# First attention: VectorE takes the row maxima two items ahead before it combines the two maps of the next item

## The chip, the cores and the metric

One core of a Trainium2 chip runs the kernel. The metric is the time of one execution on the device in microseconds; lower is better. "PE" is TensorE, "DVE" VectorE, "ACT" ScalarE, "POOL" GpSimd.

## The reference

Two transformer blocks, one after the other, on 1024 tokens of width 1024. The change is in the first one's differential attention: four heads, 1040 keys (16 meta tokens ahead of the 1024), two maps of scores with 64 dimensions each, values of 128.

```python
def diff_attention(q1, q2, k1, k2, v, lam):
    def block(args):
        q1b, q2b, start = args
        causal = k_pos[None, :] <= q_pos[:, None]
        def probs(qb, k):
            s = jnp.einsum('bhqd,bhkd->bhqk', qb, k, preferred_element_type=jnp.float32) * scale
            return jax.nn.softmax(jnp.where(causal, s, -jnp.inf), axis=-1)
        attn = probs(q1b, k1) - lam * probs(q2b, k2)
        return jnp.einsum('bhqk,bhkd->bhqd', attn, v32)
```

Around it stand normalisations, a state space branch, an output projection and a gated feed-forward part; the second block has a gating unit, a second attention with one map, and a feed-forward part of its own. None of these is changed.

## The kernel before

Each engine has its own program, and semaphores order them. The first attention is the object att1 of the class Attention (line 2108, `maps == 2`). Its work is cut into 32 items: 4 heads times 8 tiles of 128 queries. Item (h, i) has 16 + 128 (i + 1) key columns: 144 for the first tile of a head, then 272, 400, 528, 656, 784, 912 and 1040. The keys of an item are cut into tiles of 128 and one of 16, and these go in batches of up to four: items with up to three whole tiles have one batch, the next four sizes two, the longest three.

For one item n the work is, in order:

- scores: TensorE, `pe_scores` (lines 1546 and 1551, the mask), both maps, into PSUM banks 0 to 2 and 3 to 5. Each map has one place for scores, so the scores of n wait for both exponentials of n-1;
- maxima: VectorE, `dve_max` (line 1648), one TENSOR_REDUCE for each map; it waits for the scores;
- exponentials with their row sums: ScalarE, `act_exp` (line 1623), one for each map; they wait for the maxima;
- combination: VectorE, `dve_prob` (lines 1666, 1667, 1669): a reciprocal, a small product (rho), and one long instruction that adds the second map times rho to the first; it waits for both exponentials;
- turns: TensorE, `pe_turn` (line 1562), transposes a batch; the first batch of an item waits for the combination;
- copy: ScalarE, `evacuate` (lines 1609 and 1613), from PSUM to SBUF;
- product with V: TensorE, `pe_pv` (line 1576), after the copy;
- scale: VectorE, `dve_out` (line 1683), after the item's last product.

The order on each engine is written out by hand, as a loop over n. In step n TensorE does the scores of n+2, and then for each batch b of item n the turn of batch b+1 and the product of batch b; so the turn of the first batch of item n+1 comes ahead of the last product of item n. ScalarE copies the same batches, up to the first one of n+1, and then does the exponentials of n+2. VectorE does the combination of n+1, the maxima of n+2 and the scale of n. Of the 32 steps the last two have no item n+2, and the very last has no item n+1. The second attention uses the same class with one map and has no combination.

Of the kernel before, what the change touches and what calls it, by code (L numbers as in the profile page):

```python
# [66 lines left out]
def _program(nc, io, ctx):  # L67
# [286 lines left out]
    class Turn:  # L354
# [43 lines left out]
        def dve(self, v, link):  # L398
            g = self.nseg
            seg = self.width // self.nseg  # L400
            per = self.nk // 4
            n = 0
            for i in range(self.tiles + 1):
                if i < self.tiles:
                    w = self.w(i)
                    if i == 0:
                        v.wait_ge(self.sq, (self.turn + 1) * self.tiles * g)
                        rsqrt(v, link, *(t[:, 0:self.tiles, 0:g] for t in (stat, rst, tmpa, tmpb)),
                              self.nseg / self.width, EPS, self.factor)
                    if i >= 2:  # L410
                        v.wait_ge(self.turned, self.n0() + per * (i - 1))
                    for s in range(self.nseg):
                        c = slice(s * seg, (s + 1) * seg)
                        ins = v.scalar_tensor_tensor(self.xs[0:w, i % 2, c], self.src(i)[:, c],
                                                     rst[0:w, i, s:s + 1], self.gain[0:w, c], ALU.mult, ALU.mult)
                    ins.then_inc(self.scaled, 1)
                if i >= 1:
                    w = self.w(i - 1)
                    for b in range(0, self.nk, 4):
                        v.wait_ge(self.hi, self.n0() + n + 1)  # L420
                        cols = slice(self.cols(i - 1), self.cols(i - 1) + w)
                        v.tensor_tensor(self.dst(b, 1)[:, :, cols],
                                        ps[:, self.bank(n), 0:4 * w].rearrange("p (k c) -> p k c", k=4),
                                        self.dst(b, 0)[:, :, cols].bitcast(F32), ALU.subtract).then_inc(self.lo, 1)
                        n += 1
# [1033 lines left out]
    class Attention:  # L1459
# [225 lines left out]
        def dve(self, v, link):  # L1685
            N = len(self.items)
            self.dve_max(v, 0, link)
            self.dve_max(v, 1, link)
            if self.maps == 2:
                self.dve_prob(v, 0, link)  # L1690
            else:
                self.evacuate(v, nc.vector.tensor_copy, 0)
            for n in range(N):
                if self.maps == 2 and n + 1 < N:
                    self.dve_prob(v, n + 1, link)
                if n + 2 < N:
                    self.dve_max(v, n + 2, link)
                for b in self.steps(n):
                    if self.maps == 1 and b % 2 == 0:
                        self.evacuate(v, nc.vector.tensor_copy, b)  # L1700
                self.dve_out(v, n, link)
# [1213 lines left out]
```

## Time and profile before

| | |
|---|---|
| median of 3 runs | 2657.24 us (2650.01 to 2657.88) |
| the profiled execution | 2656.39 us |
| its span | 2654.6 us |
| PE busy in the span | 2442.3 us (92%) |
| DVE busy in the span | 1487.2 us (56%) |
| ACT busy in the span | 796.5 us (30%) |
| maxima of the first attention, first and last start | 304.4 and 469.9 us |
| scale of the first attention, last start | 483.1 us |

The profile is of one execution. The span runs from its first instruction to its last, and all times of rows are counted from its start. An engine's busy time leaves out its waits; TensorE's is modelled, since matmuls overlap. The granted clock of TensorE is 1.00 at 2.4 GHz and 0.50 at 1.2 GHz.

### The profile page before, as it was taken

The page shows a single profiled execution, that of the slowest core. Times are in us where ns is not written, and L with a number is a line of the kernel's source. Part 1 is how long each engine was busy: PE and PEld are TensorE (multiplying, and loading weights), DVE is VectorE, ACT ScalarE, POOL GpSimd, SP SyncE. Part 2 cuts the span into 40 slices and gives each one's busy share as a digit, 9 for nine tenths or more (in the row PEclk, how much of TensorE's full clock was granted, in tenths as well). Part 3 has the DMA queues.
Part 4 walks back from the last instruction along what each step waited for, and adds up shares of the span by engine and source line. Part 5 has one row for each costly group of instructions (what it writes and reads, how often), then busy time and mean ns, then how long its engine had stood idle before and what let it go on. Part 6 is the DMA issues. An engine that isn't in the chain of part 4 may idle for free.

```text
span 2654.6 us, 33063 instructions
## 1 busy us (share of the span) xinstructions
PE 2442.3 (92%) x11846; PEld 1983.5 (75%) x11846; DVE 1487.2 (56%) x2086; ACT 796.5 (30%) x1512; POOL 1130.1 (43%) x867
## 2 busy tenths in 40 slices
PE   8998877389799999999989999889989999999996
PEld 7976755277588888888868887677868888888885
DVE  5984656443565555655564610665555555555556
ACT  4321344513422222222233101443442222222222
POOL 3220130025365555665575424100635555655553
PEclk8998899689999999999999999999989999999998
DMA  5446410011221111111142212100321111111114
GB/s 141 123 134 163 154 40 1 4 56 56 88 60 48 47 47 59 55 51 47 48 152 92 64 32 74 62 1 1 127 68 48 48 54 54 58 47 47 50 58 143
DMA packets 177348, 179.50 MB, mean 68 GB/s; under 512 B 39752, under 2 KB 139976, under 8 KB 177248
## 3 DMA queue, kind: packets, MB, share of 16 engines
q1 hardware_dynamic: 171376, 163.96, 20.4%
q10 hardware_dynamic: 5872, 14.22, 1.6%
q8 instruction: 61, 1.00, 0.2%
q14 instruction: 39, 0.32, 0.0%
HBM read 147.65 MB, written 30.49 MB: 67 GB/s over the span
## 4 chain that ended last, share of the span: by engine, by line
PE 81%; DVE 7%; ACT 5%; issue 3%; POOL 2%; DMA 2%; SPq 0%; ACTq 0%; POOLq 0%; DVEq 0%
PE ps L267 23%; PE ps L269 22%; PE ps L268 22%; PE ps L1546 3%; PE ps L1576 3%; PE ps L1562 2%; ACT ex L1623 2%; PE ps L562 1%; DVE hbuf L513 1%; PE ps L1551 1%; DVE hbuf L2051 1%; PE ps L1437 1%; PE ps L2613 1%; PE ps L2565 1%; PE ps L1452 1%
## 5 line engine op out<-in xcount | busy, mean ns | idle before, releaser
L2051 DVE TENSOR_TENSOR hbuf<-hbuf,ps 128x1024 f32<-128x1024 f32 x320 | 390.7, 1221 | 254.0 <-PE ps L269 233.7
L207 POOL TENSOR_TENSOR wgt<-raw,ones 128x512 fp32r<-128x512 f32 x76 | 86.7, 1141 | 573.1 <-PE ps L269 418.3
L267 PE MATMUL ps<-mlp_dh,mlp_fh 128*128 128x512 f32 x672 | 264.4, 393 | 12.8 <-POOL mlp_dzl L1852 10.0
L269 PE MATMUL ps<-mlp_dh,mlp_fl 128*128 128x512 f32 x672 | 263.3, 392 | 0.0
L268 PE MATMUL ps<-mlp_dl,mlp_fh 128*128 128x512 f32 x672 | 262.7, 391 | 0.0
L1839 POOL TENSOR_TENSOR mlp_s_raw<-mlp_gh_raw,mlp_s_raw 128x512 f32<-128x512 f32 x44 | 57.2, 1299 | 284.1 <-PE ps L269 284.1
L267 PEld LDWEIGHTS ps<-mlp_dh,mlp_fh 128*128 128x128 f32 x672 | 126.6, 188 | 43.7 <-POOL mlp_dzl L1852 10.8
L268 PEld LDWEIGHTS ps<-mlp_dl,mlp_fh 128*128 128x128 f32 x672 | 126.7, 189 | 27.5
L269 PEld LDWEIGHTS ps<-mlp_dh,mlp_fl 128*128 128x128 f32 x672 | 126.5, 188 | 27.7
L1852 POOL TENSOR_TENSOR mlp_dl<-mlp_d_raw,mlp_dh 128x1024 fp32r<-128x1024 f32 x42 | 113.7, 2706 | 46.7 <-ACT mlp_dh L2028 46.7
L1546 PE MATMUL ps<-k,q 64*128 64x512 f32 (+6 forms) x416 | 89.8, 534 | 45.1 <-ACT ex L1623 43.8
L2088 DVE TENSOR_TENSOR mlp_fl<-mlp_p,mlp_fh 128x512 fp32r<-128x512 f32 x42 | 114.4, 2723 | 3.7
L209 POOL TENSOR_TENSOR wgt<-raw,wgt 128x512 fp32r<-128x512 f32 x76 | 104.2, 1371 | 6.0
L1839 POOL TENSOR_TENSOR mlp_s_raw<-mlp_gl_raw,mlp_ul 128x512 f32<-128x512 f32 x44 | 57.2, 1300 | 116.0 <-PE ps L269 116.0
L1562 PE MATMUL ps<-ident,ex 128*128 128x128 f32 (+1 forms) x464 | 82.8, 291 | 17.3 <-ACT ex L1623 14.8
L1655 DVE CUSTOM_DVE_ANT_0 ex<-ps,negc 128x128 f32<-128x128 f32 (+7 forms) x64 | 48.3, 754 | 81.2 <-PE ps L1551 80.6
L267 PE MATMUL ps<-x1h,chunk_w 128*128 128x352 f32 (+2 forms) x256 | 89.6, 350 | 2.5 <-DVE x1l L713 1.6
L1546 PEld LDWEIGHTS ps<-k,q 64*128 64x128 f32 x416 | 38.3, 199 | 69.3 <-issue 39.1
L1985 ACT CAST mlp_s3h<-mlp_s_raw 128x512 fp32r<-128x512 f32 x44 | 27.5, 625 | 202.6 <-POOL mlp_s_raw L1839 202.6
L269 PE MATMUL ps<-x1h,chunk_w 128*128 128x352 f32 (+2 forms) x256 | 87.9, 343 | 0.0
L268 PE MATMUL ps<-x1l,chunk_w 128*128 128x352 f32 (+2 forms) x256 | 87.8, 343 | 0.0
L1609 ACT COPY at<-ps 128x512 f32<-128x512 f32 (+3 forms) x96 | 43.2, 450 | 133.0 <-PE ps L1562 133.0
(485 smaller groups left out, 6812.5 us busy)
## 6 DMA issues: line engine op xcount, KB each, us to landing
h<-hbuf SPq DMA_DIRECT2D x24, 512.0 KB, 2.9
mlp_d_raw<-in_w_down SPq DMA_DIRECT2D x21, 512.0 KB, 3.5
mlp_d_raw<-in_w_ffn_out SPq DMA_DIRECT2D x21, 512.0 KB, 3.3
raw<-in_w_in SPq DMA_DIRECT2D x40, 256.0 KB, 3.0
raw<-in_w_out SPq DMA_DIRECT2D x32, 256.0 KB, 2.8
res_b<-h SPq DMA_DIRECT2D x16, 512.0 KB, 4.3
mlp_ul<-in_w_up SPq DMA_DIRECT2D x22, 256.0 KB, 3.1
mlp_uh_raw<-in_w_up SPq DMA_DIRECT2D x22, 256.0 KB, 3.4
```

The costliest lines, as they stand in the source:

```text
L207: nc.gpsimd.tensor_tensor(wh[:, s, :], r, ones[:, 0:1].broadcast_to([P, 512]), ALU.mult).then_inc(w_hi, 1)
L209: nc.gpsimd.tensor_tensor(wl[:, s, :], r, wh[:, s, :].bitcast(F32), ALU.subtract).then_inc(w_split, 1)
L267: pe.matmul(out, lhs[0], rhs[0], start=first, stop=False, skip_group_check=over)
L268: pe.matmul(out, lhs[0], rhs[1], start=False, stop=False, skip_group_check=over)
L269: return pe.matmul(out, lhs[1], rhs[0], start=False, stop=last, skip_group_check=over)
L1546: pe.matmul(self.score(item, m, a, b), self.q[rows, t, i * P:(i + 1) * P], self.k[rows, t, a:b], start=True, stop=True)
L1562: t = pe.transpose(ps[0:w, self.tbank(b), j * P:(j + 1) * P], self.ex[:, n % 3, 0, c:c + w], ident[:, :])
L1576: mm = pe.matmul(self.obank(n), self.atb[0:w, b % 3, j, :], self.v[0:w, t, h * self.dv:(h + 1) * self.dv], start=first, stop=last, skip_gr ...
L1839: nc.gpsimd.tensor_tensor(blk[name][2][:, :, :], x[:, :, :], y[:, :, :], op).then_inc(self.s["sums"], 1)
L1852: nc.gpsimd.tensor_tensor(self.d[z][1][:, :], self.d_raw[z][:, :], self.d[z][0][:, :].bitcast(F32), ALU.subtract).then_inc(self.s["split"], 1)
L2051: v.tensor_tensor(self.acc[:, i, :], self.acc[:, i, :], src, ALU.add).then_inc(self.s["added"], 1)
L2088: v.tensor_tensor(self.f[b][1][:, c], src, self.f[b][0][:, c].bitcast(F32), ALU.subtract)\
```

## The change

In step n VectorE's two calls change places: first the maxima of item n+2, then the combination of item n+1. Nothing else is changed; the second attention has no combination, and its order stays as it is.

```diff
@@ -1691,10 +1691,10 @@
             else:
                 self.evacuate(v, nc.vector.tensor_copy, 0)
             for n in range(N):
+                if n + 2 < N:
+                    self.dve_max(v, n + 2, link)
                 if self.maps == 2 and n + 1 < N:
                     self.dve_prob(v, n + 1, link)
-                if n + 2 < N:
-                    self.dve_max(v, n + 2, link)
                 for b in self.steps(n):
```

## Rows read from the trace of the kernel before

**Rows 1.** Stretches: PE, PEld, DVE, ACT, POOL busy (instructions), granted clock, DMA share, GB/s.
```profile
304.00:325.00 21.00, 15.43 (x63) 8.60 (x60) 8.93 (x23) 7.24 (x23) 0.99 (x1) 0.51 0.63 161
325.00:390.00 65.00, 45.29 (x323) 32.56 (x322) 40.64 (x72) 30.47 (x78) 29.34 (x24) 1.00 0.16 50
386.60:390.00 3.40, 1.51 (x15) 1.38 (x16) 1.62 (x4) 2.04 (x5) 0.00 (x0) 0.99 0.00 0
390.00:393.40 3.40, 3.40 (x17) 3.18 (x16) 0.69 (x3) 1.65 (x7) 0.00 (x0) 0.50 0.02 5
```

**Rows 2.** Waits from 304 to 484 us: total, times, longest.
```profile
PE ps L1546 <- ACT ex L1623: 43.8, 29, 2.7
...
DVE rl L1666 <- ACT ex L1623: 30.7, 27, 1.7
DVE negmax L1648 <- PE ps L1551: 26.9, 25, 6.0
...
PE ps L1562 <- DVE ex L1669: 2.5, 3, 1.6
ACT ex L1623 <- DVE negmax L1648: 2.2, 1, 2.2
```

**Rows 3.** The chain of waits from 404 to 475 us, shares by line.
```profile
by line: PE ps L1546 26.7%; ACT ex L1623 25.2%; issue 14.3%; PE ps L1562 12.6%; PE ps L1576 12.5%; PE ps L1551 4.4%; DVE ex L1669 1.9%; ACT at L1609 1.4%; ACT at L1613 0.8%; DVE rho L1667 0.4%; DVE rl L1666 0.3%; ACTq L1606 0.1%; DVEq L1665
```

**Rows 4.** Timeline of one round: start, duration, engine, line, operation.
```profile
418.79 0.17 DVE L1666 RECIPROCAL rl<-psum_l 128x2 f32<-128x2 f32 x1 [1.73 <-ACT ex L1623]
...
418.83 1.80 PE L1546 MATMUL ps<-k,q 64*128 64x512 f32 x8 [2.16 <-ACT ex L1623]
...
419.30 1.03 DVE L1669 SCALAR_TENSOR_TENSOR ex<-ex,rho 128x784 f32<-128x784 f32 x1
...
420.83 2.12 DVE L1648 TENSOR_REDUCE negmax<-ps 128x1 f32<-128x912 f32 x2 [0.50 <-PE ps L1551]
...
421.81 0.60 PE L1562 MATMUL ps<-ident,ex 128*128 128x128 f32 x4
...
422.93 1.03 ACT L1623 ACTIVATE ex<-ps,negmax 128x912 f32<-128x912 f32 x1
...
425.19 0.70 PE L1546 MATMUL ps<-k,q 64*128 64x512 f32 x2 [2.15 <-ACT ex L1623]
```

**Rows 5.** Timeline, the same instructions at other sizes.
```profile
433.03 1.30 DVE L1669 SCALAR_TENSOR_TENSOR ex<-ex,rho 128x1040 f32<-128x1040 f32 x1
...
434.25 0.52 DVE L1648 TENSOR_REDUCE negmax<-ps 128x1 f32<-128x144 f32 x2
...
434.47 0.60 PE L1562 MATMUL ps<-ident,ex 128*128 128x128 f32 x4
...
437.50 0.79 DVE L1648 TENSOR_REDUCE negmax<-ps 128x1 f32<-128x272 f32 x2
...
439.70 0.38 PE L1562 MATMUL ps<-ident,ex 128*128 128x128 f32 x2
...
450.93 0.61 PE L1562 MATMUL ps<-ident,ex 128*128 128x128 f32 x4
451.07 1.59 DVE L1648 TENSOR_REDUCE negmax<-ps 128x1 f32<-128x656 f32 x2 [0.34 <-PE ps L1551]
...
468.74 2.39 DVE L1648 TENSOR_REDUCE negmax<-ps 128x1 f32<-128x1040 f32 x2 [1.04 <-PE ps L1551]
...
469.84 0.60 PE L1562 MATMUL ps<-ident,ex 128*128 128x128 f32 x4
```

**Rows 6.** Timeline, scores of 656 columns and the next ones, at either clock.
```profile
407.00 2.56 PE L1546 MATMUL ps<-k,q 64*128 64x512 f32 x8 [0.60 <-ACT ex L1623]
...
413.01 1.59 PE L1546 MATMUL ps<-k,q 64*128 64x512 f32 x8 [1.27 <-ACT ex L1623]
...
449.50 1.37 PE L1546 MATMUL ps<-k,q 64*128 64x512 f32 x8 [1.31 <-ACT ex L1623]
...
453.90 0.70 PE L1546 MATMUL ps<-k,q 64*128 64x512 f32 x2 [1.27 <-ACT ex L1623]
```

## Prediction

> **What bounds the kernel now.** Only the first attention, about 304 to 484 us of the span, is touched, so I read that stretch: first the busy times and the granted clock by stretch, then the waits, the chain, and the timeline of single items. TensorE is busy for 45.29 of the 65 us from 325 to 390 [rows 1], so it is not full, and VectorE (40.64) is still less so. Nobody is short of throughput here; the stage is a ring of short waits. In the list of waits [rows 2] TensorE's scores wait for ScalarE's exponentials (43.8 us), VectorE for both (30.7 and 26.9 us). The two rows that matter most are the small ones. TensorE's turns wait for VectorE's combination 3 times, 2.5 us in all, and the exponential waits for the maxima once, 2.2 us. So today both VectorE results are nearly always ready before somebody asks. The chain of waits says the same: from 404 to 475 us scores, exponentials, turns and the product with V make it up, and VectorE's combination has 1.9% of it [rows 3].
>
> One round of the ring is in [rows 4], the step in which the scores have 912 columns and the combination 784. The exponentials of item n+1 end, and at 418.8 both TensorE (scores of n+2, to 420.8) and VectorE (reciprocal, rho, combination, 418.79 to 420.33) start. They run beside each other. VectorE then waits 0.50 us for the scores and takes both maxima, 420.83 to 422.95. Meanwhile TensorE does what is left of item n and begins at 421.81 to turn the first batch of n+1, which needs the combination; that has been ready since 420.33. ScalarE copies this batch out and at 422.93 starts the exponentials of n+2; the next scores follow at 425.19. The round takes 6.36 us. The maxima lie beside the turn and the copy, the combination beside the scores: the two VectorE parts have separate cover.
>
> **The change, part by part.** No instruction is added or removed; in each of the 30 steps that have an item n+2 the two maxima move ahead of the three combination instructions. No DMA moves, and VectorE's queue holds nothing else. What is new is a wait: VectorE takes its queue in order (in [rows 4] the maxima stand behind the combination), so the combination of n+1 now stands behind the wait for the scores of n+2 and behind both maxima. Behind the combination stand the turn of the first batch of n+1 on TensorE (with it the last product of n), its copy on ScalarE, and, queued behind that copy, the exponentials of n+2, and for these the scores of n+3 wait. The ring becomes one string: scores, maxima, combination, turn, copy, exponentials.
>
> The cost D of a step is the time by which the turn comes later. Counted from the start of the maxima it would start after M (both maxima) + 0.6 (reciprocal and rho, 418.79 to 419.30, and 0.1 of hand-overs) + P (combination), and it starts now after W:
> - 912 columns: 2.12 + 0.6 + 1.03 - (421.81 - 420.83 = 0.98) = 2.8 us [rows 4].
> - 656 columns: item n has a single batch, so the turn starts 0.14 before the maxima: 1.59 + 0.6 + 0.77 + 0.14 = 3.1 us; P is read off a line through 1.03 at 784 columns and 1.30 at 1040, 0.135 for each 128 [rows 4, 5].
> - 1040 columns: 2.39 + 0.6 + 1.17 (same line) - (469.84 - 468.74 = 1.10) = 3.1 us [rows 5].
> - 784, 528, 400 columns, M along the line from 0.52 at 144 to 2.39 at 1040: 1.86 + 0.6 + 0.90 - 0.9 = 2.5; 1.32 + 0.6 + 0.64 + 0.1 = 2.7; 1.06 + 0.6 + 0.50 + 0.1 = 2.2. (The 0.9 is W of the 912 step, a little less.)
> - 144 columns, behind the longest combination: the scores end by about 433.3 and the turn starts at 434.47 [rows 5]; 0.52 + 0.6 + 1.30 (the 1040 combination) - 1.2 = 1.2 us.
> - 272 columns, beside the longest item: TensorE has 2.2 us of work of item n (437.50 to 439.70 [rows 5]) and VectorE needs 0.79 + 0.6 + 0.36 = 1.8. This one is covered; if TensorE's work were not there it would cost 1.8.
>
> The six long sizes give 16.4 us a head, four heads 65.6; the 144 step occurs three times, 3.6. **Sum: 69 us** at the clock of today. Nothing comes back elsewhere: the wait of the scale behind the product only moves along with the ring, and the stage after it needs the finished output. W may hide 0.3 us more or less in each of the 30 steps than these few rows say: 9 us either way.
>
> **The clock.** A second term follows from the first. TensorE was at its low level (0.5, 1.2 GHz) for 304 to 325, where it waits between short items, and fell again at 390.0 after a stretch in which it was busy for only 1.51 of 3.4 us, and was low once more around 407.00 [rows 1, 6]; for 65 us between, it stayed at 1.00 (2.4 GHz) with waits of about 2.2 us a round [rows 1, 4]. The new order adds up to 3 us of waiting to almost every round with the same work. I expect it to fall often. What low costs is in [rows 6]: a round with 656 columns takes 6.01 us (407.00 to 413.01) against 4.40 (449.50 to 453.90), 1.6 more, of which the scores are 2.56 - 1.37 = 1.2 and the turn the rest, 0.4. These two stay on the string after the change; TensorE's other work is then beside VectorE's. Scores scaled by columns plus 0.4 give 0.7 (144), 1.0, 1.4, 1.6, 1.8, 2.1 and 2.3 us (1040), and 2.3 for the 272 step, where TensorE's own work is the bound: 13.2 a head, 10.2 for the first, which has no steps of 144 and 272. That is 50; the additional chunk of 16 columns at 528 and 1040 lifts it to some 53. Today it is low for 21 + 3.4 us and about 7 around 407.00 [rows 1, 6], five rounds of 6 us, 8 us of loss that the time before already holds. So: never low -8, always low 53 - 8 = +45, low for two thirds of the rounds 35 - 8 = +27. I take two thirds, nearer to low, since long gaps stand in 26 of 30 rounds; it is not all of them, since the clock also comes back: after the low scores at 407.00 those at 413.01 have more columns and take 1.59 [rows 6].
> The Trainium skill, TensorE: Matmul & The Clock Gate, section on the HAM clock gate, says that for modelling "the ramp penalty is <1% of a typical kernel span". By that this term would stay under 26 us (1% of 2654.6), and the sum would be at most 95. The row at 390.0 shows a fall in mid-stage after one thin stretch, so here it is no ramp at the start, and I don't hold to this limit.
>
> **Sum:** 69 + 27 = 96 us. The profiled execution took 2656.4 us (span 2654.6), 0.8 below the median of the runs, 2657.2. 2656.4 + 96 = 2752, say **2753 us**.
>
> **Rivals.**
> - A, the clock stays as it is: only the 69, 2726 us (at always 1.00, 2717). For it: 65 us in a row at 1.00 with gaps of 2.2 us. Against: the three falls, all at thinner work than that.
> - B, low throughout: +114, 2770 us. For it: the first 21 us show that low can hold from item to item. Against: it came back after 325 and before 413 [rows 1, 6], and the long items still give TensorE dense pieces.
> - C, more is covered than I think: with two or three batches in item n TensorE has 1 to 2 us to do, and if that work took the place of the wait, the steps of 784, 912 and 1040 would cost nothing. Left are (2.2 + 2.7 + 3.1) x 4 = 32 us, 2688. Against: W is already subtracted, and M + 0.6 + P is 3.4 to 4.2.
> - D, not slower: the maxima set the round, not the combination. Where the scores are done before the combination is (the 144 steps: ready by 433.3, taken at 434.25, 1.0 us), the maxima would come up to 1 us earlier, and if the exponential waited for them that would be gained in the seven or so steps of this kind: up to 7 us, 2650. It decides where the exponential is late by the maxima rather than by the copy ahead of it. The waits show that once in 64 exponentials, at the start [rows 2].
> - E, the change doesn't do what it says: the order on VectorE is written out instruction by instruction, and nothing in the trace has reordered it. Time unchanged, 2656.
>
> **How the numbers follow.** The clock falls for part of the rounds, 2735 to 2764 (forecast): 0.60. A 0.15, B 0.15, C 0.05, D 0.02, E 0.01, and 0.02 for a gain or a loss that I don't see. The range takes in A and B, with 5 us beyond B for its sizes and from 2717 with always 1.00 below: 2716 to 2776. What this kernel's measurement can tell from nothing is about 0.3%, 8 us. All of the forecast, A, B and C are beyond it: slower 0.96, same 0.02, faster 0.02.
>
> **What would show it.** Right: the wait of TensorE's turns for VectorE's combination grows from 2.5 us to 50 or more; VectorE's wait before the reciprocal for the exponentials (30.7) is nearly gone, and that before the maxima (26.9) grows to 60 or more; the chain of waits holds the maxima and the combination with together over 20% of the stage; the 912 round is 9.1 us at the high clock, 11 at the low; the granted clock of the stage, 0.50 now only in short pieces, is low in more than half. The stage ends at about 580 instead of 484, and all that follows is as long as before. Wrong: the exponential waiting for the maxima as often as for the copy (D), rounds of unchanged length where item n has two batches (C), or a stage of 250 us with a granted clock as before, which would put the loss in a place that I haven't named.

## The result, and the profile after

The changed kernel takes 2760.0 us (median of 4 runs, 2752.6 to 2762.3) against 2657.6 (4 runs, 2650.0 to 2659.2): 102.4 us more, ratio 1.0386, interval 1.0359 to 1.0414. The forecast was 2753 (2716 to 2776). The profiled execution took 2762.3 us, its span is 2760.4, against 2656.4 and 2654.6.

The waits of the first attention, 304 to 590 us (who waited, for whom, total, times, longest):

```profile
ACT at L1609 <- PE ps L1562: 181.8, 47, 7.7
...
DVE negmax L1648 <- PE ps L1551: 111.0, 32, 7.1
DVE o L1683 <- PE ps L1576: 74.6, 32, 3.2
PEld ps L1562 <- DVE ex L1669: 64.2, 25, 3.8
PE ps L1562 <- DVE ex L1669: 59.4, 25, 3.5
...
PE ps L1546 <- ACT ex L1623: 32.1, 30, 2.7
...
ACT ex L1623 <- DVE negmax L1648: 2.2, 1, 2.2
...
DVE rl L1666 <- ACT ex L1623: 1.0, 1, 1.0
```

Against [rows 2]: TensorE's turns wait for the combination for 59.4 us instead of 2.5, and VectorE for the scores 111.0 instead of 26.9; its wait for the exponentials ahead of the reciprocal (30.7) is gone. The exponentials wait for the maxima exactly as before, 2.2 us once: having the maxima earlier was of use to nobody.

The chain of waits of the changed kernel, 404 to 575 us:

```profile
by line: PE ps L1546 27.7%; ACT ex L1623 18.0%; issue 14.6%; PE ps L1562 11.8%; DVE negmax L1648 9.0%; DVE ex L1669 7.5%; PE ps L1576 3.9%; PE ps L1551 3.1%; DVE rho L1667 2.5%; DVE rl L1666 0.7%; ACT at L1613 0.6%; ACT at L1609 0.3%; DVEq 
```

VectorE's maxima (9.0%) are on it, which they were not at all in [rows 3], and the combination with its two small instructions has 10.7%. The time by stretches, ahead of the stage, in it and behind it (PE, PEld, DVE, ACT and POOL busy, granted clock):

```profile
0.00:309.00 309.00, 275.33 (x1611) 241.85 (x1611) 210.02 (x407) 87.31 (x164) 54.92 (x43) 0.95 0.51 141
309.00:588.00 279.00, 186.92 (x830) 122.15 (x828) 96.80 (x192) 77.28 (x209) 28.32 (x24) 0.64 0.07 24
588.00:2760.00 2172.00, 2036.60 (x9408) 1648.25 (x9408) 1177.04 (x1488) 630.50 (x1139) 1045.68 (x800) 0.97 0.19 60
```

The loss is in the stage: 279 us, where [rows 1] belong to one of 180 (304 to 484). Behind it are 2172 us against 2170. The stage begins 5 us later, though nothing ahead of it is changed; in the traces of the experiments below it begins anywhere between 303 and 312 us, so single spans are compared by the stage alone. The granted clock, 0.90 over the stage before, is 0.64.

One round, the one of [rows 4], in the changed kernel:

```profile
420.35 3.37 PE L1546 MATMUL ps<-k,q 64*128 64x512 f32 x8 [1.85 <-ACT ex L1623]
...
423.92 2.12 DVE L1648 TENSOR_REDUCE negmax<-ps 128x1 f32<-128x912 f32 x2 [5.03 <-PE ps L1551]
424.00 1.06 PE L1576 MATMUL ps<-v,at 128*128 128x128 f32 x8
...
425.95 0.15 DVE L1666 RECIPROCAL rl<-psum_l 128x2 f32<-128x2 f32 x1
426.14 0.27 DVE L1667 TENSOR_SCALAR rho<-psum_l,rl,lamv 128x1 f32<-128x1 f32 x1
426.45 1.03 DVE L1669 SCALAR_TENSOR_TENSOR ex<-ex,rho 128x784 f32<-128x784 f32 x1
427.55 1.12 PE L1562 MATMUL ps<-ident,ex 128*128 128x128 f32 x4 [2.49 <-DVE ex L1669]
...
429.18 1.03 ACT L1623 ACTIVATE ex<-ps,negmax 128x912 f32<-128x912 f32 x1
...
431.44 1.23 PE L1546 MATMUL ps<-k,q 64*128 64x512 f32 x2 [1.64 <-ACT ex L1623]
```

Each part of the string begins about where the one before it ends. The scores take 3.37 us instead of 1.80 and the turn 1.12 instead of 0.60: that is the low clock. The eight products at 424.00 take 1.06 us, as at the high clock, and the granted clock from 424.0 to 427.5 is 0.92: the fast piece of this round lies for the most part in TensorE's wait. Between them VectorE works alone from 425.1 on while TensorE waits 2.49 us, which is the order. From scores to scores it is 11.09 us against 6.36.

For all comparisons below I use the length of a round: from the end of an item's second row sum (ScalarE's ACTIVATION_READ_ACCUMULATOR of line 1623) to that of the next item. It repeats to some hundredths from the second to the fourth head where the clock is the same; the first head has an effect of its own, told at the end. Columns are the score widths; the third head unless said otherwise, L where TensorE was at 0.50 for a part of the round:

```
                              144    272    400    528    656    784    912    1040   31 rounds
before (fourth head)          4.01   5.04   3.42   4.47   4.39   5.82   6.36   7.37     166.4
changed                       5.57L  5.03   5.92L  8.80L  9.12L 10.13L 11.06L 12.68L    268.7
e1 wait only                  5.65L  5.04   4.71   6.39L  7.78L  8.25L  8.64L  8.16     215.0
e2 one map ahead              5.41L  5.03   5.09L  8.19L  8.37L  8.82L  8.48L 10.71L    241.3
e7 changed + dummies          5.65L  5.03   5.58   7.07   7.42   8.24   9.07  10.35     231.6
e8 only 656 (fourth head)     4.77L  5.39L  3.42   4.92L  9.12L  8.03L  8.00L  7.37     195.4
e9 only 656 + dummies         4.01   5.04   3.42   4.47   7.41   5.82   6.36   8.94L    183.9
e5 exponentials first         3.06   4.22   3.44   4.24   4.34   4.90   5.46   6.91     149.6
e6 e5 + maxima first          6.40L  5.28   3.30   6.42L  8.21L  9.47L  8.19L 11.15L    220.4
e10 e5 + dummies              3.06   4.22   3.45   4.23   4.34   4.90   5.46   6.91     146.1
```

### The profile page after: what moved, and what is told of

The parts are those of the page before. It is cut to its first block, busy times and chain, and to the rows that moved or that the text cites. A ratio compares the mean times of both kernels' runs of the same rounds, so it can differ in the third digit from the quotient of the medians.

```text
span 2760.4 us, 33063 instructions
## 1 busy us (share of the span) xinstructions
PE 2498.8 (91%) x11846; PEld 2012.2 (73%) x11846; DVE 1483.9 (54%) x2086; ACT 795.1 (29%) x1512; POOL 1128.9 (41%) x867
## 4 chain that ended last, share of the span: by engine, by line
PE 79%; DVE 9%; ACT 5%; issue 3%; DMA 2%; POOL 2%; SPq 0%; ACTq 0%; POOLq 0%; DVEq 0%
PE ps L267 22%; PE ps L269 21%; PE ps L268 21%; PE ps L1546 4%; PE ps L1562 2%; PE ps L1576 2%; ACT ex L1623 2%; DVE hbuf L513 1%; PE ps L562 1%; DVE negmax L1648 1%; DMA msb<-ssm_lags 1%; DVE ex L1669 1%; PE ps L1551 1%; DVE hbuf L2051 1%; PE ps L2613 1%
## 5 line engine op out<-in xcount | busy, mean ns | idle before, releaser
L1562 PE MATMUL ps<-ident,ex 128*128 128x128 f32 (+1 forms) x464 | 93.5, 320 | 74.4 <-DVE ex L1669 59.4
L1546 PE MATMUL ps<-k,q 64*128 64x512 f32 (+6 forms) x416 | 116.4, 672 | 33.4 <-ACT ex L1623 32.1
L1562 PEld LDWEIGHTS ps<-ident,ex 128*128 128x128 f32 (+1 forms) x464 | 58.7, 162 | 82.1 <-DVE ex L1669 64.2
L1648 DVE TENSOR_REDUCE negmax<-ps 128x1 f32<-128x144 f32 (+7 forms) x64 | 46.6, 769 | 111.0 <-PE ps L1551 111.0
L1546 PEld LDWEIGHTS ps<-k,q 64*128 64x128 f32 x416 | 47.7, 249 | 68.1 <-issue 44.2
```

Source lines behind the costliest of these rows:

```text
L1546: pe.matmul(self.score(item, m, a, b), self.q[rows, t, i * P:(i + 1) * P], self.k[rows, t, a:b], start=True, stop=True)
L1562: t = pe.transpose(ps[0:w, self.tbank(b), j * P:(j + 1) * P], self.ex[:, n % 3, 0, c:c + w], ident[:, :])
L1648: v.tensor_reduce(negmax[:, n % 3, m:m + 1], self.score(n, m, 0, w), AX.X, ALU.max, negate=True).then_inc(self.s[f"max{m}"], 1)
```

## The experiments

The times of the kernel before beside them had medians of 2658.1 us (e1 to e4), 2656.7 (e5 to e8) and 2657.0 (e9 and e10).

**e1, the wait without the maxima.** The order of before, but the combination waits for the scores of n+2:

```diff
                 if self.maps == 2 and n + 1 < N:
+                    for m in range(2 if n + 2 < N else 0):
+                        v.wait_ge(self.s[f"s{m}"], n + 3)
                     self.dve_prob(v, n + 1, link)
```

> VectorE keeps the order of before (combination, then maxima), but the combination of item n+1 now waits for the scores of item n+2, as it has to in the changed order. This leaves the wait in and takes the maxima out of the string. Theory (each instruction ahead of the turn adds its length): of the 69 us of the reordering the maxima are some 43 (M summed over 30 steps), so about 26 us remain at the clock of before, and with TensorE at its low clock for a part of the rounds 30 to 50 in all: 2687 to 2707. Rival (the wait for the scores is what hurts, the maxima are covered by TensorE's other work): nearly the whole 100 us, 2750. Rival (only the maxima hurt): no change, 2657.

Measured: 2707.4 us, ratio 1.0188 (1.0165 to 1.0210), +49.3. VectorE waits 91.7 us for the scores, now ahead of the reciprocal. It is at the upper edge of the expectation (2707), and both rivals fall: the wait alone is half of the loss, and with the maxima on the string comes the other half. The clock, low for about 106 us of the stage where it was low for about 30 before, is in it: at 1.00 the 1040 round costs 0.79 more than before and the 400 round 1.29 (by the terms of the prediction without M, 0.7 and 1.2).

**e2, the maxima of one map ahead.** The loop calls the maxima of map 0, then the combination, then the maxima of map 1:

```diff
...
+                if self.maps == 2 and n + 2 < N:
+                    self.dve_max(v, n + 2, link, (0,))
                 if self.maps == 2 and n + 1 < N:
                     self.dve_prob(v, n + 1, link)
                 if n + 2 < N:
-                    self.dve_max(v, n + 2, link)
+                    self.dve_max(v, n + 2, link, (1,) if self.maps == 2 else None)
```

> Only the maxima of the first map go ahead of the combination; those of the second map stay behind it. Theory: half of the maxima, 21 us, leaves the string, and a little low clock with it: 75 to 85 us over before, 2732 to 2742. Rival (order matters only as whether anything stands ahead of the combination): as the change, 2760. Rival (the second map's maxima now become the last thing ahead of the exponentials and take the place of what was saved): also near 2760, and the trace would show the exponential waiting for the maxima.

Measured: 2733.1 us, ratio 1.0282 (1.0260 to 1.0304), +75.1, as the theory has it. Wait alone, one map, two maps: 49, 75, 102 us. Each map's maxima ahead of the combination cost 26 to 27 us, with the low clock that they bring.

**e3, the changed kernel with TensorE kept busy.** 14 dummy products ahead of the scores (not in the first step, and not ahead of scores of 144 columns) and, in each step, 22 ahead of the turn of the next item's first batch:

```diff
+        def pe_fill(self, pe, n, count):
...
+            for _ in range(count):
+                pe.matmul(ps[:, 5 + 2 * (n % 2), 256:256 + P], identb[:, :], maskb[:, :], start=True, stop=True,
+                          skip_group_check=True)
...
```

In items of several batches the 22 dummies stand between the products of one sum, and each of them starts a new sum in the bank of that sum: the output of the item is then not the right one. The work and its order are those described.

> The changed kernel, and in each step TensorE does 22 dummy products of 128 columns (bfloat16, into free columns of the output's bank) ahead of the turn of the next item's first batch and 14 ahead of the scores, where it waits anyway; nobody reads them. They keep TensorE busy and should keep its clock at 1.00. Theory (order 69 us at the clock of before, or 61 over a kernel that is always at 1.00, and the rest clock): the stage at 1.00 and 55 to 70 us over before, 2713 to 2727. Rival A (the low clock costs nothing, TensorE's slower work lies beside waits): as the change, 2755 to 2765, though the clock is at 1.00. Rival B (the clock is most of the loss): under 2690.

Measured: 2736.7 us, ratio 1.0304 (1.0274 to 1.0334), +78.7: outside the expectation, though faster than the changed kernel. The rounds say why. In the third head those of 400, 528, 656, 784 and 1040 columns were at 0.99 or 1.00 (5.57, 7.08, 7.41, 8.24, 10.36); the 912 round was still low for a part in three of four heads (10.6 to 11.6), and in the 272 round (6.66 instead of 5.03) TensorE was busy without a pause, at 1.00: there the dummies themselves stood in the way. A test with faults of its own; e7 mends them.

**e4, the kernel before with 14 dummies ahead of the scores.** The same function, called ahead of the scores alone, with the same exceptions.

> The kernel before, with 14 such dummy products ahead of the scores of each step. Theory: the short low pieces of before go away, 8 us faster, 2649, if the dummies fit into the waits of 1.1 to 2.2 us (at the low clock they take 1.5 us and can hold up a short round). Rival: the dummies delay the scores and eat the gain, 2657 to 2665.

Measured: 2658.4 us, ratio 1.0008 (0.9995 to 1.0022): no change, the rival's case. The 528 and 656 rounds that had been low in the third head (4.93, 6.01) are at 4.47 and 4.39, but the 272 rounds grew from about 5.04 to 5.42 and more, and the 144 rounds of the second and fourth head from 4.44 and 4.01 to 5.61 and 4.91, with a clock of 0.70 and 0.66. Dummies placed this way get nothing of the 8 us.

**e5, exponentials ahead of the copy.** VectorE's order of before; on ScalarE:

```diff
+                ahead = self.maps == 2 and n + 2 < len(self.items)
                 for b in self.steps(n):
+                    if ahead and b == self.first[n + 1]:
+                        self.act_exp(act, n + 2)
...
-                if n + 2 < len(self.items):
+                if n + 2 < len(self.items) and not ahead:
                     self.act_exp(act, n + 2)
```

> VectorE's order of before; on ScalarE the exponentials of item n+2 go ahead of the copy of the first batch of item n+1 (they stood behind it). The exponentials then wait for the maxima alone. Theory (the ring before the change is set by turn and copy, the maxima have about 0.6 to 1 us to spare): the 912 round falls from 6.36 to about 5.4 us, scores 2.0 + first maximum 1.1 + two exponentials 2.2, and the stage by 15 to 25 us: 2633 to 2643. Rival (TensorE's products, which now get their copy later, become the bound): no gain, 2655 or more.

Measured: 2638.3 us, ratio 0.9930 (0.9904 to 0.9956), 18.4 us faster than before. Its 912 round, 5.46 us long (lines are 3 later here):

```profile
371.85 1.80 PE L1546 MATMUL ps<-k,q 64*128 64x512 f32 x8 [1.25 <-ACT ex L1623]
...
372.32 1.03 DVE L1672 SCALAR_TENSOR_TENSOR ex<-ex,rho 128x784 f32<-128x784 f32 x1
...
373.85 2.12 DVE L1651 TENSOR_REDUCE negmax<-ps 128x1 f32<-128x912 f32 x2 [0.50 <-PE ps L1551]
...
374.83 0.60 PE L1562 MATMUL ps<-ident,ex 128*128 128x128 f32 x4
375.06 1.02 ACT L1623 ACTIVATE ex<-ps,negmax 128x912 f32<-128x912 f32 x1 [0.51 <-DVE negmax L1651]
```

The exponential starts 1.2 us after the maxima have started, with the first map's result and before the turn is copied; in [rows 4] it was 2.1. Here, other than in the kernel before, the exponentials wait for the maxima (36.3 us in 28 waits, 306 to 470 us).

**e6, the same with VectorE's changed order.**

> The same edit on ScalarE, with VectorE's changed order (maxima first). This makes true what the not-slower rival of the prediction needed, exponentials that wait for the maxima and not for the copy. Rival D: then maxima first is no loss, or a small gain against the same kernel with the order of before. Theory: the turn still waits for the combination, which stands behind scores and maxima (912: 2.0 + 2.1 + 1.6, then the turn, 6.4 us a round or more), and the next scores stand behind it on TensorE, so it stays slower than the kernel with the order of before by 25 to 60 us, 2665 to 2700; better than the changed kernel, since copy and exponentials are out of the string.

Measured: 2715.8 us, ratio 1.0227 (1.0199 to 1.0254), 77 us slower than e5. So maxima first loses even where the exponentials wait for the maxima and not for the copy of the turn; the not-slower rival falls though its condition is met. What it named is there, but small: the 400 rounds, and from the second head on only these, are shorter than in e5, 3.30 against 3.44 at 1.00. From its waits, 310 to 540 us:

```profile
DVE negmax L1651 <- PE ps L1551: 67.6, 31, 4.8
DVE o L1686 <- PE ps L1576: 65.8, 32, 3.2
...
PE ps L1562 <- DVE ex L1672: 56.4, 26, 3.0
ACT ex L1623 <- DVE negmax L1651: 45.2, 24, 4.6
```

The turn waits for the combination as in the changed kernel (56.4 against 59.4 us), and the scores of the next round are queued behind it on TensorE. The result is 16 us above my upper bound. TensorE was at the low clock for some 137 us where it was for some 20 in e5, and the expectation had no term for that, so a part of the 77 us is clock; how large a part wasn't measured. That the order costs without it too shows in the 528 round of the second head, at 1.00 in both: 5.31 against 4.24.

**e7, dummies placed by size.** 40 ahead of the turn from 400 columns on, 16 ahead of the scores from 528 on, and those ahead of the turn without starting a new sum.

> The changed kernel with dummy products placed by size: 40 ahead of the turn where the scores have 400 columns and more, 16 ahead of the scores where they have 528 and more, none in the rounds of 144 and 272 (in the first version the dummies themselves lengthened these by 1 to 1.6 us, and the 912 round still fell to the low clock). Theory: all rounds of 400 columns and more as the order term alone has them, 5.6, 7.1, 7.5, 8.3, 9.1 and 10.4 us, and 58 to 65 us over before, 2716 to 2723. Rival (the dummies hold up the turn, and with fewer of them it would be faster): rounds longer than the first version's 5.57, 7.07, 7.42, 8.24 and 10.35.

Measured: 2719.0 us, ratio 1.0237 (1.0208 to 1.0266), +62.3, and the six round lengths as the theory has them in the second to fourth head. Not all is at 1.00: in the first head the 400 round took 8.82, with the dummies at the low clock, and in the second the 272 round 6.63 at 0.74. The 912 round at 1.00 (here the dummies' function moves the maxima to line 1662):

```profile
403.70 1.80 PE L1546 MATMUL ps<-k,q 64*128 64x512 f32 x8 [1.16 <-ACT ex L1637]
...
405.70 2.12 DVE L1662 TENSOR_REDUCE negmax<-ps 128x1 f32<-128x912 f32 x2 [3.77 <-PE ps L1551]
...
408.24 1.03 DVE L1683 SCALAR_TENSOR_TENSOR ex<-ex,rho 128x784 f32<-128x784 f32 x1
...
409.33 0.66 PE L1562 MATMUL ps<-ident,ex 128*128 128x128 f32 x4 [0.26 <-DVE ex L1683]
...
412.77 1.99 PE L1546 MATMUL ps<-k,q 64*128 64x512 f32 x8 [1.15 <-ACT ex L1637]
```

Scores 1.80 again and turn 0.66, and still 9.07 us from scores to scores: what remains over 6.36 is the order, 2.7. The turn waits 0.26 us for the combination, so the dummies ahead of it had ended and didn't hold it up.

**e8 and e9, maxima ahead in the four 656 steps alone,** without and with dummies in these steps:

```diff
+                early = self.maps == 2 and n + 2 < N and self.items[n + 2][1] == 4
+                if early:
+                    self.dve_max(v, n + 2, link)
                 if self.maps == 2 and n + 1 < N:
                     self.dve_prob(v, n + 1, link)
-                if n + 2 < N:
+                if n + 2 < N and not early:
                     self.dve_max(v, n + 2, link)
```

> Maxima ahead of the combination only in the four steps whose scores have 656 columns; all others keep the order of before. Theory: these four rounds go from 4.39 to 7.5 us if the clock holds and to about 9.1 where it falls, and the neighbours stay as they are but for what low clock they inherit: 12 to 25 us in all, 2669 to 2682. Rival (the loss of one round is made good in the next, where work waits ready): the neighbours shorter than 4.47 and 5.82 us.

Measured, in a single run: 2688.0 us, +31, more than expected. The 656 rounds took 7.9 to 9.1, but in three heads (the second to the fourth) the next two rounds, in which nothing is changed, went from 5.82 to about 8.0 and from 6.36 to about 8.0. Their stretches in the second head, the 656, 784, 912 and part of the 1040 round:

```profile
373.00:382.20 9.20, 6.00 (x22) 4.05 (x22) 2.96 (x6) 2.17 (x5) 0.00 (x0) 0.51 0.00 0
382.20:390.20 8.00, 5.82 (x25) 3.83 (x25) 3.57 (x8) 2.64 (x6) 0.00 (x0) 0.71 0.00 0
390.20:398.20 8.00, 5.84 (x28) 3.44 (x29) 3.96 (x7) 3.01 (x7) 0.00 (x0) 0.79 0.00 0
398.20:405.00 6.80, 5.23 (x37) 3.63 (x37) 4.32 (x6) 2.89 (x6) 0.00 (x0) 1.00 0.01 1
```

> The kernel with maxima ahead of the combination in the four 656 steps alone, with 16 and 40 dummy products in those four steps and nowhere else. In its version without them the 656 rounds took 7.9 to 9.1 us, and the two unchanged rounds behind them 7.4 to 8.0 and 8.0 where 5.82 and 6.36 are usual. Theory (the neighbours only inherit a low clock): 656 rounds of 7.42 us, 784 and 912 rounds back at 5.82 and 6.36, and 12 to 14 us over before, 2669 to 2672. Rival (the later turn pushes work into the next rounds): the neighbours stay 1.5 to 2 us long though the clock is at 1.00, 2680 or more.

Measured: 2672.9 us, ratio 1.0062 (1.0044 to 1.0079), +16.0, a little more than the 12 to 14 expected. The 656 rounds are at 7.42 in three heads, and behind them 784 is at 5.82 in those three: the neighbours had inherited the clock and no work. In each of these heads the clock still falls one or two rounds later (912 at 7.98 or 1040 at 8.94, and behind the latter the 144 round at 5.22), and in the first head the 784 and 1040 rounds are low for a part; these falls are the likely place of the rest over 12.

**e10, e5 with 10 dummies ahead of the scores of 912 and 1040 columns.**

> Exponentials ahead of the copy, VectorE's order of before, and 10 dummy products ahead of the scores of 912 and 1040 columns. In three of four heads the 1040 round fell to the low clock and took 8.4 to 8.6 us, 6.91 in the one where it didn't. Theory: all at 6.91, 4 to 5 us faster than without the dummies, 2634. Rival (the dummies themselves take the 0.5 us a round that they were to save, or the clock falls elsewhere): 2637 to 2641.

Measured: 2634.9 us, ratio 0.9914 (0.9898 to 0.9931), 22.1 us faster than before. All 1040 rounds are at 6.91, which is 4.8 us less in all than in e5; elsewhere the clock fell once, in the 528 round of the second head (5.14 instead of 4.24 us, at 0.67), as the rival had it. It is the fastest version of this study; between it and e5 there are 3.5 us, with intervals that overlap, and the sum of the rounds is shorter by the same 3.5.

## Why the prediction was right

**The order term, 69 us: measured 67.** The rounds at 1.00 of e7 (third head) minus those of before, against D of the prediction: 2.16 (2.2) at 400 columns, 2.60 (2.7), 3.03 (3.1), 2.42 (2.5), 2.71 (2.8), 2.98 (3.1) at 1040; together 15.9 a head, 63.6 if all four heads are alike. The 144 round at 1.00 is 5.17 (e7, second head) against 4.01: 1.16 (1.2), three times 3.5. The 272 round is 5.04 before and 5.03 or 5.04 after: the one step that I called covered is covered. The parts of the sum are as argued too: e1 and e2 take the maxima out of the string one map at a time. One thing comes back that I had put at nothing: from the last exponentials to the last scale the changed kernel needs 7.7 us instead of 10.2.

**The clock term, 27 us: measured 35.** The 31 rounds grew by 268.7 - 166.4 = 102.3 us, of which 67 are the order. TensorE was low for 197 of the 268.7 us, 73%, where I had taken two thirds of the rounds. Low cost 1.73 us at 528 columns (I had 1.4), 1.70 at 656 (1.6), 1.9 at 784 (1.8), 2.0 at 912 (2.1) and 2.3 at 1040 (2.3), all as changed minus e7. Three small sizes were too high: the 272 round, for which I had 2.3, was at 1.00 in the changed kernel (TensorE works without a pause from 381.3 to 385.2 in it); the 400 round, low for a part only, lost 0.3 outside the first head where I had 1.0; and the 144 round lost 0.4 (0.7). What was too low was the share: every round from 528 columns on was low in every head, for all of it or a part, and these are the dear ones. By these prices low clock takes 10.4 us in each of the last three heads and about 11 in the first, some 42 in all where two thirds of my 53 gave 35; the kernel before loses 9 of them too (I had 8). The last 1.5 of the 35 are not clock at all but two combinations beside GpSimd in the first head, told below. That errors of both signs met is luck; the mechanism isn't. e7 against the changed kernel is the direct test: the same order, 41 us faster with TensorE kept busy. So rival A with its figure for a clock that always holds (2717) is what the order costs alone (e7: 2719), and the clock doesn't hold; rival B (low throughout, 2770) missed the result by 10 us, my own 2753 by 7.
The Trainium skill (TensorE: Matmul & The Clock Gate, section on the HAM clock gate) would have had this term under 1% of the span. These 41 us are 1.5% of 2760, so here the limit doesn't hold: the page's sentence is about one ramp, and this kernel leaves 1.00 in each head anew.

**C fell** with the 784, 912 and 1040 rounds, which lost 2.4 to 3.0 us each at 1.00. **D fell** twice: in the changed kernel the exponentials wait for the maxima as little as before, and in e6, where they do wait for them, the kernel is still 77 us slower than with the order of before. **E** was never at issue: VectorE's list of instructions shows the two groups exchanged.

**Of the signs:** the turns' wait (50 or more: 59.4), VectorE's two waits (nearly gone: 1.0; 60 or more: 111.0), the 912 round (9.1 at the high clock: 9.07, seen in e7; 11 at the low: 11.06) and the clock (low in more than half: 73%) came as written. The share of maxima and combination in the chain was to be over 20% and is 19.7 (404 to 575 us); the stage was to end at 580 and ended at 588, 5 of it for the later start.

## What to carry to other kernels

When engines pass work round in a ring, moving an instruction ahead of another on its engine pays only if somebody waits for it: the waits said who (turns for the combination, exponentials for a copy), and the maxima were wanted by nobody. Moving them put two parts that had separate cover into one string and lengthened nearly every round by the whole of both, less what TensorE had left to do. Count then what the longer wait does to TensorE's clock, beyond the changed round as well; and where the first in line waits behind something that it doesn't need, as the exponentials did behind the copy, that is the move that pays.

## What was not expected of the hardware

One longer wait can cost more in its neighbours than in itself. In e8 four rounds made 3 us longer (in the last three heads TensorE waits 2.76 to 2.81 us once in each) brought 12 us by themselves and nearly 20 by the clock, in good part in rounds whose waits of about 2.2 us had held 1.00 in the kernel before [rows 1, 4]. Whether the clock falls is thus a matter of what came just before, and single rounds with the same wait are found at either level: unchanged 784 rounds behind a 656 round take 7.8 to 8.0 us in e8 and 5.82 in e9, where dummies filled the 656 round.

The combination can take twice its time while GpSimd works: in the changed kernel's first head the one of 400 columns takes 1.30 us and the maxima just ahead of it, with 528 columns, the usual 1.32:

```profile
325.61 1.32 DVE L1648 TENSOR_REDUCE negmax<-ps 128x1 f32<-128x528 f32 x2 [3.40 <-PE ps L1551]
...
327.34 1.30 DVE L1669 SCALAR_TENSOR_TENSOR ex<-ex,rho 128x400 f32<-128x400 f32 x1
```

In the other heads, beside an idle GpSimd, it takes 0.64. GpSimd was splitting weights at that time, without a gap:

```profile
327.18 1.04 POOL L207 TENSOR_TENSOR wgt<-raw,ones 128x512 fp32r<-128x512 f32 x1
328.30 1.48 POOL L209 TENSOR_TENSOR wgt<-raw,wgt 128x512 fp32r<-128x512 f32 x1
```

The combination has two inputs in SBUF, the maxima one in PSUM. The Trainium skill (VectorE: DVE Perf Modes, section on two Vector instructions with no wait between them) mentions that a second SBUF read interface of VectorE is shared with GpSimd; the rows agree, but no run here took GpSimd's work away. GpSimd pays as well, by who comes first: its instruction at 328.30, behind the start of the combination, has 1.48 us where most of its kind have 1.26, and at 347.39 it is the combination that keeps its time (0.90 at 656 columns) while GpSimd's next takes 1.83. In the kernel before, the longer combination was hidden beside the scores; in the changed order it is on the string, 0.7 us in the 528 round of the first head, which is what that round has over the others (9.47 against 8.80), and 0.8 in the 656 round (9.89 against 9.12, the combination 1.54 instead of 0.77).
